# Gate and up products of four feed-forwards as seven half-size block products in place of eight, with the activations kept in float32 until the down product

## The chip, the cores and the metric

The kernel runs on one NeuronCore of one Trainium2 chip. A core has TensorE (PE, with its weight loads as PEld), VectorE (DVE), ScalarE (ACT), GpSimd (POOL), SyncE (SP, which here only issues DMAs) and 16 DMA engines. The engines run their own instruction queues in order and wait for each other by semaphores. The metric is the time of one execution on the device, in microseconds (us).

## What is computed

A gMLP layer and a dilated-attention layer are followed by a two-layer block whose four feed-forwards are called (layer, i): (0, 0), (0, 1), (1, 0), (1, 1). With T = 512 tokens, D = 1024 features and a hidden width of 2816 each feed-forward is

```python
def swiglu(x, w_gu, w_down):
    g, u = jnp.split(x @ w_gu, 2, axis=-1)      # w_gu: 1024 x 5632
    return (jax.nn.silu(g) * u) @ w_down        # w_down: 2816 x 1024

x = layer_norm_2(DN_ALPHA * x + 0.5 * swiglu(x, ffn_w_gu[layer, 0], ffn_w_down[layer, 0]), ...)
```

Attention mixers (mla after (0, 0), nsa after (1, 0)) stand between them, and a small stage of compressed keys and values stands between (0, 1) and (1, 0). All is float32.

## The kernel before, in words

**Products.** Every large product is made of matmuls on pairs "high" and "low": the high part is the value rounded to TensorE's fp32r form (written by ScalarE with `ACT.Copy`), the low part is value minus high (written by VectorE with a subtract). `mm3` issues three matmuls for one 128 x 128 weight tile: high x high, low x high, high x low. The stationary operand of a matmul is loaded anew each time.

**Weights.** `weight_panels` lists all weights as panels of up to 128 x 2048 in the order in which they are used. SP loads panel g into `RAW[g % 2]` once panel g - 2 has been split (L585). `prepare(g)` on ScalarE (L1330) and VectorE (L1710) splits panels in order into a ring of two homes (`w_high`, `w_low`), or, for the panels next to a row stage, into `edge_high`, `edge_low`.

**A feed-forward.** `xt_high` and `xt_low` hold the tokens' features turned, 8 tiles of 128 features x 512 tokens. The gate columns come in five chunks of 512 (two panels each: 4 output tiles x 8 feature tiles x 3 = 96 matmuls of 512 tokens), each followed by the up chunk of the same size; a last pair of panels ("last") holds 256 gate and 256 up columns. ScalarE takes silu of a gate bank into `gate_rows` (L1582), VectorE multiplies it with the up bank (L2070), ScalarE writes `hidden_high` (L1588) and VectorE `hidden_low` (L2073) at once. `down` multiplies them with 11 panels of the down weights.

**Starts.** Before a feed-forward stands a row stage: 4 tiles of 128 tokens are normalised, turned by TensorE and split. In three of the four feed-forwards `edge_product` begins the first product on the first 256 tokens with matmuls of 256 columns (L607 to L610), while the later tiles are still in work; 96 such matmuls come after the last tile is split (`xt_ready` of tile 3). Feed-forward (1, 0) follows the compressed stage instead: its first product runs whole, then `compress_out` issues a few small matmuls, and TensorE waits for ScalarE's copy of their result (`cmp_kept`, L1658).

**Order.** No scheduler: the program text of each engine's block is its order. GpSimd before only issues DMAs, takes roots of single columns (L2265) and scales a bias (L2383).

## Time and profile before

| What | Value |
|---|---|
| Time, median of 3 runs | 2964.39 us (2963.52 to 2964.39) |
| Span of the profiled execution | 2961.8 us |
| TensorE busy | 2919.8 us, 99% |
| Weight loads busy | 2421.4 us, 82% |
| VectorE busy | 1227.6 us, 41% |
| ScalarE busy | 1047.1 us, 35% |
| GpSimd busy | 101.4 us, 3% |
| Chain that ended last | 92% on TensorE |

The span of the profiled execution is 2.6 us under the median of the runs; no other time is given for it. Busy time is the time in which at least one instruction of the engine is in flight; matmuls overlap, so the cost of one in a stream is the distance between starts, not its own duration.

### The profile page before, as it was taken

To read this page: it belongs to the slowest core of one execution; us is meant where nothing else is said; L and a number is where in the kernel's file an instruction comes from. 1 tells how busy PE (TensorE), PEld (TensorE's weight loads), DVE (VectorE), ACT (ScalarE), POOL (GpSimd) and SP (SyncE) were. 2 spreads that over 40 slices of the span, in tenths; PEclk is the share of its full clock that TensorE was granted. 3 is DMA by queue.
4 is the path that set the end of the run, shared out by engine and by line. 5 is a ranking of instruction groups with operands and counts; after the bars stand their busy time and mean duration, and the time that the engine had idled before them with its cause. 6 is when DMAs were issued, how large, how long until landed. Compare 5 with 4: busy or idle time off the path is not lost.

```text
span 2961.8 us, 35864 instructions
## 1 busy us (share of the span) xinstructions
PE 2919.8 (99%) x15356; PEld 2421.4 (82%) x15356; DVE 1227.6 (41%) x1703; ACT 1047.1 (35%) x1749; POOL 101.4 (3%) x153
## 2 busy tenths in 40 slices
PE   7999999999999999999999999999999999999998
PEld 6888888788888788888868888888888886788887
DVE  4364342343333743333664333162332458633223
ACT  3323333444444332222473222133222248532221
POOL 1000000020000000000100000010000011000000
PEclk9999999999999999999999999999999999999999
DMA  5432322222222233323303323253332330123321
GB/s 195 140 102 95 102 89 99 84 67 79 79 80 75 93 99 100 99 93 101 95 23 107 100 86 99 100 145 114 100 100 100 80 106 1 58 100 100 100 100 71
DMA packets 145261, 278.18 MB, mean 94 GB/s; under 512 B 29578, under 2 KB 45114, under 8 KB 144976
## 3 DMA queue, kind: packets, MB, share of 16 engines
q1 hardware_dynamic: 136064, 247.17, 26.0%
q0 software_dynamic: 9040, 28.73, 3.0%
q8 instruction: 121, 1.98, 0.3%
q14 instruction: 36, 0.29, 0.0%
HBM read 271.56 MB, written 4.25 MB: 93 GB/s over the span
## 4 chain that ended last, share of the span: by engine, by line
PE 92%; DVE 4%; ACT 1%; issue 1%; DMA 1%; POOL 0%; SPq 0%; POOLq 0%; DVEq 0%; ACTq 0%
PE bank L596 26%; PE bank L598 26%; PE bank L597 26%; PE bank L734 2%; PE bank L607 1%; PE bank L610 1%; PE bank L609 1%; PE bank L822 1%; PE bank L790 1%; PE bank L754 1%; PE bank L806 1%; PE bank L743 1%; PE bank L715 1%; PE bank L968 0%; DMA cmp_pos_t<-in_cmp_pos 0%
## 5 line engine op out<-in xcount | busy, mean ns | idle before, releaser
L1710 DVE TENSOR_TENSOR w_low<-raw,w_high 128x2048 fp32r<-128x2048 f32 (+2 forms) x213 | 481.5, 2260 | 1190.4 <-ACT w_high L1330 1184.2
L596 PE MATMUL bank<-xt_high,w_high 128*128 128x512 f32 x2040 | 803.0, 394 | 1.6 <-DVE w_low L1710 1.2
L598 PE MATMUL bank<-xt_high,w_low 128*128 128x512 f32 x2040 | 794.7, 390 | 0.0
L597 PE MATMUL bank<-xt_low,w_high 128*128 128x512 f32 x2040 | 794.1, 389 | 0.0
L1330 ACT ACTIVATE w_high<-raw 128x2048 fp32r<-128x2048 f32 (+2 forms) x213 | 402.1, 1888 | 896.6 <-PE bank L598 892.3
L596 PEld LDWEIGHTS bank<-xt_high,w_high 128*128 128x128 f32 x2040 | 382.4, 187 | 89.5 <-issue 10.0
L598 PEld LDWEIGHTS bank<-xt_high,w_low 128*128 128x128 f32 x2040 | 382.3, 187 | 81.4
L597 PEld LDWEIGHTS bank<-xt_low,w_high 128*128 128x128 f32 x2040 | 382.7, 188 | 77.5
L596 PE MATMUL bank<-w_high,hidden_high 128*128 128x512 f32 x640 | 249.3, 390 | 0.0
L598 PE MATMUL bank<-w_high,hidden_low 128*128 128x512 f32 x640 | 249.0, 389 | 0.0
L597 PE MATMUL bank<-w_low,hidden_high 128*128 128x512 f32 x640 | 249.0, 389 | 0.0
L598 PEld LDWEIGHTS bank<-w_high,hidden_low 128*128 128x128 f32 x640 | 120.2, 188 | 25.1
L596 PEld LDWEIGHTS bank<-w_high,hidden_high 128*128 128x128 f32 x640 | 120.1, 188 | 24.9
L597 PEld LDWEIGHTS bank<-w_low,hidden_high 128*128 128x128 f32 x640 | 120.2, 188 | 24.7
L596 PE MATMUL bank<-w_high,xt_high 128*128 128x512 f32 (+1 forms) x336 | 131.0, 390 | 0.3 <-DVE w_low L1710 0.3
L597 PE MATMUL bank<-w_low,xt_high 128*128 128x512 f32 (+1 forms) x336 | 129.2, 384 | 0.0
L598 PE MATMUL bank<-w_high,xt_low 128*128 128x512 f32 (+1 forms) x336 | 129.2, 384 | 0.0
L1588 ACT ACTIVATE hidden_high<-gate_rows 128x512 fp32r<-128x512 f32 x88 | 55.1, 630 | 154.7 <-DVE gate_rows L2070 154.7
L2070 DVE TENSOR_TENSOR gate_rows<-bank,gate_rows 128x512 f32<-128x512 f32 x88 | 60.7, 689 | 115.5 <-PE bank L598 115.5
L1582 ACT ACTIVATE gate_rows<-bank 128x512 f32<-128x512 f32 x88 | 52.3, 598 | 151.7 <-PE bank L598 125.2
L2265 POOL TENSOR_TENSOR small<-small 128x1 f32<-128x1 f32 (+1 forms) x43 | 25.2, 585 | 2109.1 <-DVE small L1736 2070.8
L596 PEld LDWEIGHTS bank<-w_high,xt_high 128*128 128x128 f32 x336 | 79.4, 236 | 8.7 <-issue 1.1
(367 smaller groups left out, 3766.4 us busy)
## 6 DMA issues: line engine op xcount, KB each, us to landing
raw<-in_ffn_w_gu SPq DMA_DIRECT2D x80, 1024.0 KB, 5.1
raw<-in_ffn_w_down SPq DMA_DIRECT2D x44, 1024.0 KB, 5.0
raw<-in_b_w_in SPq DMA_DIRECT2D x40, 1024.0 KB, 5.1
raw<-in_a_w_in SPq DMA_DIRECT2D x24, 1024.0 KB, 5.2
raw<-in_a_w_out SPq DMA_DIRECT2D x8, 1024.0 KB, 5.0
raw<-in_ffn_w_gu SPq DMA_DIRECT2D x16, 512.0 KB, 4.8
raw<-in_w_out SPq DMA_DIRECT2D x5, 1024.0 KB, 4.9
raw<-in_w_mem_kv SPq DMA_DIRECT2D x4, 1024.0 KB, 5.2
```

The source lines that it names most:

```text
L596: pe.matmul(o, lh, rh, start=start, stop=False, skip_group_check=True)
L597: pe.matmul(o, lh, rl, start=False, stop=False, skip_group_check=True)
L598: return pe.matmul(o, ll, rh, start=False, stop=stop, skip_group_check=True)
L607: pe.matmul(o[:, cols], lh, rh[:, cols], start=a == 0 and i == 0 and kk == 0, stop=False, skip_group_check=True)
L609: pe.matmul(o[:, cols], lh, rl[:, cols], start=False, stop=False, skip_group_check=True)
L610: ins = pe.matmul(o[:, cols], ll, rh[:, cols], start=False, stop=a == 1 and i == 1 and kk == 3, skip_group_check=True)
L734: ins = pe.matmul(ps[4 + m % 2][:, a:b], q, k, start=True, stop=True)
L1330: act.activation(homes[n][0][:, 0:w], RAW[n % 2][:, 0:w], ACT.Copy).then_inc(sem["w_high_ready"], step("w_high_ready", n))
L1582: act.activation(G[:, j, :], ps[j][:], ACT.Silu).then_inc(sem["gate_read"], step("gate_read", (f, c, j)))
L1588: ins = act.activation(HTH[:, 4 * c + j, :], G[:, j, :], ACT.Copy)
L1710: dve.tensor_tensor(homes[n][1][:, 0:w], RAW[n % 2][:, 0:w], homes[n][0][:, 0:w].bitcast(F32), ALU.subtract).then_inc(sem["w_low_ready"], ...
L2070: dve.tensor_tensor(G[:, j, :], ps[bank + j][:], G[:, j, :], ALU.mult).then_inc(sem["up_read"], step("up_read", (f, c, j)))
```

## The change

The first 256 hidden columns of each feed-forward are computed as before (panels "first", moved from the end to the front). Each further unit of 256 hidden columns (10 units, `UNITS` = 11) takes the product of the unit's gate and up weights with the tokens as a 2 x 2 block product: the tokens cut in features 0 to 511 and 512 to 1023 and in tokens 0 to 255 and 256 to 511; the weights cut in the same feature halves and in gate and up. Seven block products of half size (`FACTORS`) in place of eight give the four result blocks. For that:

- four sums and differences of token blocks are made once per feed-forward (three on VectorE, sum 3 on GpSimd in `differences`), and split into high and low;
- four differences of weight blocks are made in every unit on GpSimd (`put`), two of them in place in `RAW`, so a panel stays there until they are made and split;
- each of the seven weight factors (128 x 1024) is split by `high(q)` on ScalarE and `low(q)` on VectorE into one of five slots, used again once the product five earlier is done;
- products add to each other in three PSUM banks per unit; ScalarE copies a bank between two products (snapshot), VectorE adds snapshots and banks, silu and the multiplication follow in halves of 256 tokens;
- the hidden activations stay in float32 and are split after the units, from the last unit on (`hidden_high(u)`, `hidden_low(u)`).

The core of the diff:

```diff
-        for c in range(5):
-            deep(("gate", l, i, c), w, 512 * c, 512)
-            deep(("up", l, i, c), w, D_FF + 512 * c, 512)
         for k0 in (0, 4):
-            add(("last", l, i), [(0, 4, 512, 256, rows(w, k0, 4, 2560, 256)),
-                                 (256, 4, 512, 256, rows(w, k0, 4, D_FF + 2560, 256))])
+            add(("first", l, i), [(0, 4, 512, 256, rows(w, k0, 4, 0, 256)),
+                                  (256, 4, 512, 256, rows(w, k0, 4, D_FF, 256))])
+        for u in range(1, UNITS):
+            for c0 in (256 * u, D_FF + 256 * u):
+                add(("unit", l, i, u), [(0, 8, 256, 256, rows(w, 0, 8, c0, 256))])
...
+        g, up = ids["unit", *f, u]
+        gate_raw, up_raw = RAW[g % 2], RAW[up % 2]
+        slot = FFN[f]["slots"][q % 5]
+        src = (gate_raw[:, 0:1024], gate_raw[:, 1024:2048], DIFF2, gate_raw[:, 0:1024], up_raw[:, 0:1024],
+               up_raw[:, 1024:2048], DIFF4)[n]
...
+    DIFF2, DIFF4 = (SPARE[i][:, 0:4, 256:512] for i in range(2))
...
+            if g - 2 in unit_of:
+                l, i, u, half = unit_of[g - 2]
+                sp.wait_ge(sem["factor_ready"], at("factor_ready", ((l, i), u, 5 if half else 3)))
+                if half == 0:
+                    sp.wait_ge(sem["differences"], at("differences", ((l, i), u, 6)))
...
+            moving = (tokens(0, 0), tokens(4, 0), sums(2), sums(1), sums(3), sums(4), tokens(4, 256))
+            for q in range(FACTORS * (UNITS - 1)):
+                u, n = 1 + q // FACTORS, q % FACTORS
+                A, B, C = unit_banks(u)
+                bank = (A, B, A, C, A, C, A)[n]
+                pe.wait_ge(sem["factor_ready"], at("factor_ready", (f, u, n)))
+                if n == 0 and u >= 3:
+                    pe.wait_ge(sem["unit_gated"], at("unit_gated", (f, u - 2, 1)))
...
+                    pe.wait_ge(sem["snapped"], at("snapped", (f, u, n - 2)))
+                if u == 1 and 2 <= n < 6:
+                    pe.wait_ge(sem["sum_split"], at("sum_split", (f, SUM_ORDER[n - 2])))
+                slot = tiles["slots"][q % 5]
+                for j in range(2):
+                    o = bank[:, 256 * j:256 * j + 256]
+                    for kk in range(4):
+                        a = 256 * kk + P * j
+                        opens = n in (0, 1, 3) and j == 0 and kk == 0
+                        ins = mm3(o, slot[:, a:a + P], slot[:, 1024 + a:1024 + a + P], *moving[n](kk), opens,
+                                  n in (1, 5, 6) and j == 1 and kk == 3)
+                ins.then_inc(sem["unit_done"], step("unit_done", (f, u, n)))
...
+            def high(q):
...
+                g, up = ids["unit", l, i, u]
+                if n in (0, 1):
+                    act.wait_ge(sem[f"panel_loaded{g % 2}"], at(f"panel_loaded{g % 2}", g))
+                elif n == 5:
+                    act.wait_ge(sem[f"panel_loaded{up % 2}"], at(f"panel_loaded{up % 2}", up))
+                else:
+                    act.wait_ge(sem["differences"], at("differences", (f, u, n)))
+                if q < 5:
+                    act.wait_ge(sem["product_done"], at("product_done", ("panel", tiles["before"][q])))
+                else:
+                    act.wait_ge(sem["unit_done"], at("unit_done", (f, 1 + (q - 5) // FACTORS, (q - 5) % FACTORS)))
+                act.activation(dst, src, ACT.Copy).then_inc(sem["factor_high"], step("factor_high", (f, u, n)))
...
+            prepare(ids["first", l, i][-1])
+            high(0)
+            high(1)
+            for n in SUM_ORDER:
+                if n == 3:
+                    act.wait_ge(sem["sum3_ready"], at("sum3_ready", f))
+                else:
+                    act.wait_ge(sem["sum_ready"], at("sum_ready", (f, n)))
+                act.activation(tiles["sum_high"][n][:], tiles["sum"][n][:],
+                               ACT.Copy).then_inc(sem["sum_high"], step("sum_high", (f, n)))
+            for j in range(2):
+                act.wait_ge(sem["product_done"], at("product_done", ("acc", ("first", l, i), j)))
+                act.activation(SNAP[j][:].rearrange("p a n -> p (a n)"), ps[j][:], ACT.Silu).then_inc(sem["gate_read"], step("gate_read", (f, j)))
+            high(3)
...
+                    to, bank = {0: (0, A), 2: (1, A), 3: (3, C), 4: (2, A)}[n]
+                    act.activation(SNAP[to][:].rearrange("p a n -> p (a n)"), bank[:],
+                                   ACT.Copy).then_inc(sem["snapped"], step("snapped", (f, u, n)))
+                if n == 2:
+                    act.wait_ge(sem["gate_summed"], at("gate_summed", (f, u)))
+                    act.activation(SNAP[0][:], SNAP[0][:], ACT.Silu).then_inc(sem["unit_gated"], step("unit_gated", (f, u, 0)))
+                if n == 6:
...
+                def x(high, k0, t0):
...
+                dve.wait_ge(sem["xt_ready"], at("xt_ready", (s, TT - 1)))
+                s1, s2, s4 = (tiles["sum"][n][:] for n in (1, 2, 4))
+                link(dve.tensor_tensor(s1, x(True, 0, 256), x(True, 4, 256), ALU.add))
+                link(dve.tensor_tensor(s1, s1, x(False, 0, 256), ALU.add))
+                end(1, s1, x(False, 4, 256), ALU.add)
+                link(dve.tensor_tensor(s2, s1, x(True, 0, 0), ALU.subtract))
+                end(2, s2, x(False, 0, 0), ALU.subtract)
+                link(dve.tensor_tensor(s4, x(True, 4, 0), s2, ALU.subtract))
+                end(4, s4, x(False, 4, 0), ALU.add)
...
+            token_sums()
+            for n in SUM_ORDER:
+                dve.wait_ge(sem["sum_high"], at("sum_high", (f, n)))
+                dve.tensor_tensor(tiles["sum_low"][n][:], tiles["sum"][n][:], tiles["sum_high"][n][:].bitcast(F32),
+                                  ALU.subtract).then_inc(sem["sum_split"], step("sum_split", (f, n)))
...
+                    dve.wait_ge(sem["unit_done"], at("unit_done", (f, u, n)))
+                if n == 1:
+                    dve.wait_ge(sem["snapped"], at("snapped", (f, u, 0)))
+                    dve.tensor_tensor(SNAP[0][:], bank(B), SNAP[0][:], ALU.add).then_inc(sem["gate_summed"], step("gate_summed", (f, u)))
+                if n == 5:
+                    dve.wait_ge(sem["snapped"], at("snapped", (f, u, 2)))
+                    link(dve.tensor_tensor(SNAP[1][:], bank(C), SNAP[1][:], ALU.add))
+                    dve.wait_ge(sem["unit_gated"], at("unit_gated", (f, u, 0)))
+                    dve.tensor_tensor(tiles["hidden"][u][:, :, 0:256], SNAP[1][:], SNAP[0][:],
+                                      ALU.mult).then_inc(sem["unit_hidden"], step("unit_hidden", (f, u, 0)))
+                    dve.wait_ge(sem["snapped"], at("snapped", (f, u, 4)))
+                    link(dve.tensor_tensor(SNAP[2][:], SNAP[2][:], SNAP[3][:], ALU.add))
+                if n == 6:
...
-        prepare(ids["gate", 1, 0, 0][-1] + 1)
+        prepare(ids["first", 1, 0][-1])
         dve.wait_ge(sem["kv_kept"], at("kv_kept"))
-        ffn(1, 0)
+        dve.wait_ge(sem["cmp_halves_done"], at("cmp_halves_done"))
+        ffn(1, 0, "l02")
...
+            high, low, out = XTH, XTL, FFN[f]["sum"][3][:]
+            pool.wait_ge(sem["xt_ready"], at("xt_ready", (s, TT - 1)))
+            link(pool.tensor_tensor(out, high[:, 0:4, 0:256].bitcast(F32), high[:, 0:4, 256:512].bitcast(F32), ALU.subtract))
+            link(pool.tensor_tensor(out, out, low[:, 0:4, 0:256].bitcast(F32), ALU.add))
+            pool.tensor_tensor(out, out, low[:, 0:4, 256:512].bitcast(F32),
+                               ALU.subtract).then_inc(sem["sum3_ready"], step("sum3_ready", f))
...
+            for u in range(1, UNITS):
+                g, up = ids["unit", l, i, u]
+                b11, b21 = deep(RAW[g % 2][:, 0:1024]), deep(RAW[g % 2][:, 1024:2048])
+                b12, b22 = deep(RAW[up % 2][:, 0:1024]), deep(RAW[up % 2][:, 1024:2048])
+                def put(n, dst, a, b):
+                    pool.tensor_tensor(dst, a, b, ALU.subtract).then_inc(sem["differences"], step("differences", (f, u, n)))
+                    pool.wait_ge(sem["differences"], at("differences", (f, u, n)))
...
+                pool.wait_ge(sem["factor_ready"], at("factor_ready", (f, u, 0)))
+                put(3, b11, b12, b11)
+                if u == 1:
+                    pool.wait_ge(sem["product_done"], at("product_done", ("panel", ids["first", l, i][1])))
+                    pool.wait_ge(sem["sum_ready"], at("sum_ready", (f, 1)))
+                else:
+                    pool.wait_ge(sem["factor_ready"], at("factor_ready", (f, u - 1, 2)))
+                put(2, DIFF2, b22, b11)
+                put(4, b12, b22, b12)
+                if u > 1:
+                    pool.wait_ge(sem["factor_ready"], at("factor_ready", (f, u - 1, 6)))
+                put(6, DIFF4, b21, DIFF2)
```

**Start of (1, 0), ScalarE.** In the program before, the rows from the copy of the compressed keys (`cmp_keys`) on are:

```order
L1657 ACTIVATE cmp_keys<-bank 128x32 [waits cmp_done]
L1658 ACTIVATE cmp_values<-bank 128x128
L1582 ACT_TABLE_LOAD [waits product_done]
L1582 ACTIVATE gate_rows<-bank 128x512 [waits kv_kept]
L1582 ACTIVATE gate_rows<-bank 128x512 [waits product_done] x3
L1330 ACTIVATE w_high_63<-raw_62 128x2048 [waits product_done,panel_loaded1]
```

In the changed program they are:

```order
L1838 ACTIVATE cmp_keys<-bank 128x32 [waits cmp_done]
L1839 ACTIVATE cmp_values<-bank 128x128
L1712 ACTIVATE w_high_63<-raw_61 128x1024 [waits product_done,panel_loaded0,kv_kept]
L1712 ACTIVATE w_low_65<-raw_61 128x1024 [waits product_done,panel_loaded0]
L1730 ACTIVATE sum_high_161<-sum_10_163 128x1024 [waits sum_ready]
L1730 ACTIVATE sum_high_164<-sum_10_166 128x1024 [waits sum_ready]
L1730 ACTIVATE sum_high_167<-sum_10_169 128x1024 [waits sum3_ready]
L1730 ACTIVATE sum_high_170<-sum_10_172 128x1024 [waits sum_ready]
L1734 ACT_TABLE_LOAD
L1734 ACTIVATE snapshot_253<-bank 128x512 [waits product_done]
L1734 ACTIVATE snapshot_254<-bank 128x512 [waits product_done]
```

`raw_61` here is the gate panel of unit 1 (factors 0 and 1), `sum_...` are the token sums in the order 2, 1, 3, 4, and L1734 is the silu of the gate banks of the first product. The split of factor 0 stands right behind the compressed stage's copies, and the sums' splits stand between it and the first silu.

**The same place, VectorE.** Before, behind the compressed stage:

```order
L1710 TENSOR_TENSOR w_low_66<-raw_61,w_high_64 128x2048 [waits w_high_ready]
L1710 TENSOR_TENSOR w_low_65<-raw_62,w_high_63 128x2048 [waits w_high_ready,kv_kept]
L1710 TENSOR_TENSOR w_low_66<-raw_61,w_high_64 128x2048 [waits w_high_ready]
L2070 TENSOR_TENSOR gate_rows<-bank,gate_rows 128x512 [waits gate_read,product_done] x4
L2073 TENSOR_TENSOR hidden_low<-gate_rows,hidden_high 128x2048 [waits hidden_high]
```

In the changed program:

```order
L1894 TENSOR_TENSOR edge_low_kv<-raw_61,edge_high_kv 128x2048 [waits w_high_ready]
L1894 TENSOR_TENSOR w_low_66<-raw_62,w_high_64 128x2048 [waits w_high_ready]
L2249 TENSOR_TENSOR w_high_63<-raw_61,w_high_63 128x1024 [waits factor_high,cmp_halves_done,kv_kept]
L2249 TENSOR_TENSOR w_low_65<-raw_61,w_low_65 128x1024 [waits factor_high]
L2265 TENSOR_TENSOR sum_10_166<-xt_high 128x1024 [waits xt_ready]
L2266 TENSOR_TENSOR sum_10_166<-sum_10_166,xt_low 128x1024 [waits dve_step]
L2260 TENSOR_TENSOR sum_10_166<-sum_10_166,xt_low 128x1024 [waits dve_step]
L2268 TENSOR_TENSOR sum_10_163<-sum_10_166,xt_high 128x1024 [waits sum_ready]
L2260 TENSOR_TENSOR sum_10_163<-sum_10_163,xt_low 128x1024 [waits dve_step]
L2270 TENSOR_TENSOR sum_10_172<-xt_high,sum_10_163 128x1024 [waits sum_ready]
L2260 TENSOR_TENSOR sum_10_172<-sum_10_172,xt_low 128x1024 [waits dve_step]
L2284 TENSOR_TENSOR sum_low_162<-sum_10_163,sum_high_161 128x1024 [waits sum_high,sum_ready]
```

The seven sums (L2260 to L2270) stand behind the low parts of factors 0 and 1, each of which waits for its high part (`factor_high`), which ScalarE writes in the rows above.

**Within a unit, GpSimd.** Before, nothing stands here. In the changed program each unit has four rows, and the fifth is the next unit's first:

```order
L2555 TENSOR_TENSOR raw_62<-raw_61,raw_62 128x1024 [waits factor_ready,panel_loaded0,differences]
L2555 TENSOR_TENSOR xt_spare_54<-raw_61,raw_62 128x4x256 [waits factor_ready,differences]
L2555 TENSOR_TENSOR raw_61<-raw_61 128x1024 [waits differences]
L2555 TENSOR_TENSOR xt_spare_55<-raw_62,xt_spare_54 128x4x256 [waits factor_ready,differences]
L2555 TENSOR_TENSOR raw_62<-raw_61,raw_62 128x1024 [waits factor_ready,panel_loaded0,differences]
```

These are `put(3)`, `put(2)`, `put(4)`, `put(6)`: `raw` are the unit's gate and up panels, `xt_spare` the spare places DIFF2 and DIFF4. The first waits for the up panel and for factor 0's low part.

## Rows read from the trace of the kernel before

**Rows 1.** The page: busy us, share of the span, instructions.
```profile
span 2961.8 us, 35864 instructions
...
PE 2919.8 (99%) x15356; PEld 2421.4 (82%) x15356; DVE 1227.6 (41%) x1703; ACT 1047.1 (35%) x1749; POOL 101.4 (3%) x153
```

**Rows 2.** Windows, gate and up of (0, 0): us, PE, PEld, DVE, ACT, POOL, clock, DMA.
```profile
1085.00:1262.00 177.00, 177.00 (x783) 146.61 (x782) 56.17 (x36) 51.36 (x49) 0.00 (x0) 1.00 0.30 95
```

**Rows 3.** Timeline, TensorE, 512 columns: start us, us, what; 24 starts apart.
```profile
1100.06 0.39 PE L596 MATMUL bank<-xt_high,w_high 128*128 128x512 f32 x1
...
1105.50 0.39 PE L596 MATMUL bank<-xt_high,w_high 128*128 128x512 f32 x1
```

**Rows 4.** Timeline, TensorE, 256 columns, 83 starts apart, and one weight load.
```profile
1060.84 0.28 PE L607 MATMUL bank<-xt_high,edge_high_s 128*128 128x256 f32 x1
...
1070.79 0.28 PE L610 MATMUL bank<-xt_high,edge_low_s 128*128 128x256 f32 x1
...
1070.67 0.19 PEld L610 LDWEIGHTS bank<-xt_high,edge_low_s 128*128 128x128 f32 x1
```

**Rows 5.** Groups by form, ScalarE and VectorE: busy us, mean ns, idle before.
```profile
L1330 ACT ACTIVATE w_high<-raw 128x1024 fp32r<-128x1024 f32 x2 | 2.1, 1057 | 0.0
...
L1582 ACT ACTIVATE gate_rows<-bank 128x512 f32<-128x512 f32 x88 | 52.3, 598 | 151.7 <-PE bank L598 125.2 <-PE bank L610 26.5
...
L1710 DVE TENSOR_TENSOR w_low<-raw,w_high 128x1024 fp32r<-128x1024 f32 x2 | 2.4, 1220 | 0.0
...
L2070 DVE TENSOR_TENSOR gate_rows<-bank,gate_rows 128x512 f32<-128x512 f32 x88 | 60.7, 689 | 115.5 <-PE bank L598 115.5
...
L2031 DVE TENSOR_TENSOR b_o<-b_o,b_o 128x512 f32<-128x512 f32 x8 | 5.5, 692 | 0.3
```

**Rows 6.** The page, DMA issues: KB each, median us to landing.
```profile
raw<-in_ffn_w_gu SPq DMA_DIRECT2D x80, 1024.0 KB, 5.1
...
raw<-in_ffn_w_gu SPq DMA_DIRECT2D x16, 512.0 KB, 4.8
```

**Rows 7.** Groups by form, GpSimd, whole span.
```profile
L2265 POOL TENSOR_TENSOR small<-small 128x1 f32<-128x1 f32 x40 | 22.1, 552 | 2023.4 <-DVE small L1736 1985.0 <-DVE small L1743 38.3
...
L2383 POOL TENSOR_SCALAR n_bias<-nsa_dist 128x512 f32<-128x512 f32 x12 | 18.4, 1539 | 113.9 <-DVE small L1889 100.2 <-PE bank L610 13.4
```

**Rows 8.** The same in 2440 to 2520; VectorE in 2450.7 to 2452.6, in 2519 to 2525.
```profile
L2383 POOL TENSOR_SCALAR n_bias<-nsa_dist 128x512 f32<-128x512 f32 x8 | 12.5, 1562 | 100.3 <-DVE small L1889 100.2
...
L1903 DVE TENSOR_SCALAR n_p<-n_p,small,nsa_gates 128x128 f32<-128x128 f32 x2 | 1.3, 633 | 0.0
...
L1903 DVE TENSOR_SCALAR n_p<-n_p,small,nsa_gates 128x128 f32<-128x128 f32 x2 | 0.7, 344 | 0.0
```

**Rows 9.** Timeline, start of feed-forward (0, 0): VectorE, TensorE.
```profile
1061.80 1.29 DVE L1729 TENSOR_TENSOR xt_low<-bank,xt_high 128x512 fp32r<-128x512 f32 x2 [2.45 <-ACT xt_high L1343]
...
1074.75 0.28 PE L610 MATMUL bank<-xt_high,edge_low_s 128*128 128x256 f32 x1
...
1074.87 0.40 PE L596 MATMUL bank<-xt_high,w_high 128*128 128x512 f32 x1
```

**Rows 10.** Timeline, start of feed-forward (1, 0): TensorE, ScalarE.
```profile
2023.66 1.10 PE L1242 MATMUL bank<-cmp_w_t,cmp_hidden 128*128 128x64 f32 x8
...
2025.22 0.50 PE L596 MATMUL bank<-xt_high,w_high 128*128 128x512 f32 x1 [0.46 <-ACT cmp_values L1658]
...
2024.90 0.27 ACT L1658 ACTIVATE cmp_values<-bank 128x128 f32<-128x128 f32 x1
...
2025.19 1.28 ACT L1582 ACT_TABLE_LOAD   x1
```

**Rows 11.** Windows around an idle TensorE, columns as in rows 2.
```profile
410.00:415.00 5.00, 2.35 (x11) 1.59 (x9) 3.09 (x4) 3.06 (x5) 0.55 (x1) 1.00 0.00 0
...
415.00:420.00 5.00, 4.73 (x18) 3.96 (x19) 3.68 (x7) 2.98 (x7) 0.55 (x1) 0.66 0.00 0
```

More of the change, by code:

```diff
@@ L371, in build @@
             freed_by[g] = ids[y][-5 if len(ids[y]) > 4 else -4]
-    ring = [g for g in range(len(panels)) if g not in homes]
+    home("kv", ids["first", 1, 0][0], 28, 36)
+    freed_by[ids["first", 1, 0][0]] = ids["kv_a"][1]
+    unit_of = {g: (l, i, u, half) for (l, i) in FFN for u in range(1, UNITS)
+               for half, g in enumerate(ids["unit", l, i, u])}
+    ring = [g for g in range(len(panels)) if g not in homes and g not in unit_of]
     for n, g in enumerate(ring):
@@ L1040, in ffn @@
-            product(("last", l, i), 4, [(ps[setA[j]][:], feature(512, j * P, XTH, XTL)) for j in range(4)],
-                    lambda j: pe.wait_ge(sem["gate_read"], at("gate_read", (f, 4, j))))
+            tiles = FFN[f]
+            jobs = [(ps[setA[j]][:], feature(512, j * P, XTH, XTL)) for j in range(4)]
+            if s:
+                edge_product(("first", l, i), jobs, s)
+            else:
+                product(("first", l, i), 4, jobs, lambda j: None, ahead=ahead)
+            if between:
+                between()
@@ L1593, in _ @@
+            for u in range(3, UNITS):
+                hidden_high(u)
         ffn(0, 0)
```

271 lines of the change are left out of this document (201 added, 70 removed).

## The prediction

> **What bounds the kernel now.** I read the page first: TensorE is busy for 2919.8 of 2961.8 us, VectorE for 41% of the span, GpSimd for 3% [rows 1]. Then a window inside the gate and up products of (0, 0): 177 us, TensorE busy for all of it, clock 1.00, VectorE and ScalarE each busy for under a third [rows 2]. So in these stages matmuls alone set the time, and what a matmul costs is the distance from one start to the next. The timeline gives it: with 512 columns 24 starts take 5.44 us, 226.7 ns each [rows 3]; with 256 columns, in the edge products, 83 starts take 9.95 us, 119.9 ns each, every matmul with a fresh weight load of 0.19 us that overlaps its neighbours [rows 4]. The reader should see that two halves cost 239.8 ns where one whole costs 226.7: halving a matmul is not free, and the gain of seven products for eight is first cut by that.
>
> **TensorE in the units.** A unit of 256 hidden columns now takes 4 output tiles x 8 feature tiles x 3 = 96 matmuls of 512 columns, 96 x 226.7 ns = 21.76 us. In the changed kernel it takes 7 products x 2 x 4 x 3 = 168 of 256 columns, 168 x 119.9 ns = 20.14 us. That is 1.62 us less, not the eighth of 2.7 us. There are 10 units in each of 4 feed-forwards: -64.8 us. The first 256 columns and the down product keep their matmuls. One block product lasts 24 x 119.9 ns = 2.88 us.
>
> **Splits and sums within a unit, costed at nothing.** ScalarE: seven high parts of 1024 at 1.06 us and six PSUM reads or silus at 0.60 us, 11.0 us of 20.14. VectorE: seven low parts at 1.22 us and five adds or multiplications of 512 at 0.69 us, 12.0 us [rows 5]. Both fit beside TensorE. The tight place is the snapshot: the bank of product n goes on being added to in product n + 2, so ScalarE has one product, 2.88 us, to wake and copy it in 0.60 us; its longest other task in that time is a silu and a high part, 1.66 us. It holds. A factor's slot comes free four products ahead of its use, 11.5 us for 0.60 + 1.06 + 1.22 us of work. The hidden splits left for the end (eight low parts, 9.8 us of VectorE) lie beside the first two down panels, 48 matmuls x 226.7 ns = 10.9 us each. The panels land in 5.1 us; pieces whose rows are 256 columns long already exist and land in 4.8 us for half the size, two to a panel [rows 6], so I keep 5.1.
>
> **GpSimd, the new cover that can fail.** Each unit has four `put`, and they close a loop: four puts, then SP may load the next gate panel (5.1 us), then high and low of factor 0 (1.06 + 1.22 us), and only then the next unit's first put. With 0.8 us that I allow for six semaphores between, the loop is 4p + 8.2 us. It is hidden while it is under 20.14 us, so p may be up to 3.0 us. No row shows a GpSimd tensor_tensor of 1024 elements. The nearest rows are 0.55 us for one element and 1.54 us for 512 with one input [rows 7]: 1.94 ns for an element, 2.54 us for 1024. Below, p can't be under the 1.54 us of half the size; above, if two inputs cost twice the slope, 4.5 us. I take 2.54, the same line continued, 2.6 with its own semaphore: the loop is 18.6 us and hidden. At 4.5 us it would be 26.2 us, and the kernel some 210 us slower than now. The Trainium skill (GPSIMD Engine Reference, Elementwise — side-by-side cycle accounting) gives 4497 ns for 2048 float32 elements with two inputs; halving what is over the one-element 0.55 us is an estimate of 2.5 us, and the sum by it is the same.
>
> What VectorE and GpSimd do to each other is to be seen in the nsa stage. Four short VectorE operations on 128 elements last 633 ns beside a GpSimd bias scaling and 344 ns without one; GpSimd's own mean is 1562 ns there against 1539 ns over all [rows 7, 8]. So VectorE gives way by 0.29 us an operation and GpSimd hardly. Within a unit VectorE has 8 us to spare, and nothing more is charged.
>
> **The three starts behind a row stage.** At the start of (0, 0) VectorE ends the last split of tokens at 1063.1 and TensorE's 96 matmuls of 256 columns run to 1074.8, 11.7 us later [rows 9]. In the changed kernel two block products follow (5.8 us), and the third needs, from VectorE and in this order: two low parts, seven sums of 1024 each waiting for the one before (1.22 us and 0.07 that I allow for each semaphore, 9.0), four low parts of sums, two multiplications, two low parts. That is 8 x 1.22 + 9.0 + 1.4 = 20.2 us against 17.5 of TensorE's: 2.7 us of stall. GpSimd makes sum 3 and its first put in these 10 us; at 0.29 us for each of eight VectorE operations that is 2.3 us more. I take 5.0 us for each, 15 us.
>
> **The start of (1, 0).** Here ScalarE's program has the split of factor 0 behind the compressed stage's copies, which end at 2025.2, the moment at which TensorE now goes on with the up product [rows 10]. The tokens have been ready long before, but VectorE's sums are queued behind the low part of factor 0, and ScalarE's first silu behind all sum splits. From 2025.2 on: high 1.06, the same 20.2 us on VectorE, 21.3 us, against 5.8 us of TensorE's work: 15.5 us of stall. In it TensorE idles from about 5.2 to 15.5 us for the silu (sums to 12.5, high part 1.1, a table load of 1.28, silu 0.6) and product 1 follows. After a stretch of 5 us with TensorE at 2.35 us of work the granted clock is 0.66 in the next 5 us [rows 11], between its two levels of 1.2 and 2.4 GHz; most of that falls inside the wait. With 1 us for it and 1 us for GpSimd's company: 17.5 us.
>
> **Sum.** -64.8 + 15 + 17.5 = -32.3 us. Profiled span and median differ by 2.6 us [rows 1], which doesn't change: 2964.4 - 32.3 = 2932 us.
>
> **The rivals.**
> - GpSimd's loop decides (3 in 10). For it: the whole loop has 1.5 us of slack, p is read off a one-input operation, and while puts run VectorE has low parts with two inputs in SBUF, which rows 8 don't show. If each put has to let half or all of a 1.22 us operation pass, p is 3.2 to 3.8 us and the unit 21.0 to 23.4 us. From p = 3.2 on the gain is gone (40 x (21.0 - 21.76) + 32.5 = about 0); at 3.5 us the unit is 22.2 us and the kernel 40 x 0.44 + 32.5 = 50 us slower, 3014 us. Against it: GpSimd's mean in rows 8. The Trainium skill (SBUF — State Buffer, Who interferes with whom) says that a VectorE instruction with two SBUF inputs contends with a GpSimd instruction that reads SBUF; no row here shows that pair.
> - The starts are covered (1 in 10): if the chained sums follow closer and sum splits overlap, the three starts cost about 1 us each and only (1, 0) stays, at some 10 us: 2964.4 - 64.8 + 13 = 2913 us, 2900 at the least. Against it: the order on VectorE is fixed, and 20.2 us is pure work.
> - The starts cost more (1 in 10): if VectorE's sums are slowed by half beside GpSimd, 5 us more each, 20 us in all: 2952 us.
> - That matmuls of 256 columns from `unit_slot` cost other than those of the edges: each ns is 168 x 40 = 6.7 us. Rows 4 show the same shapes and forms; it is inside the range.
>
> **How the numbers follow.** The forecast has 5 in 10 and its own range is 2918 to 2945 us. What a measurement of this kernel tells from no change is about 0.2%, 6 us. Of GpSimd's 3 in 10 a tenth of a chance (0.03) ends faster, 0.03 the same, 0.24 slower; of the dear starts 0.02 the same. Faster 0.71, same 0.05, slower 0.24. The range reaches down into the covered starts and up to p = 3.5: 2903 to 3012 us; outside are 0.12 of GpSimd's case and some 0.05 below and between.
>
> **What the profile after would show.** Starts of L664 to L666 119.9 ns apart; a unit every 20.1 us with TensorE busy throughout (if it is 21 us or more, the chain of waits should name GpSimd's L2555 or the gate panel's load in front of ScalarE's high part of factor 0); GpSimd's puts at 2.5 to 2.7 us; three gaps of 3 to 5 us before the third block product, and one of 15 to 18 us in two pieces after the compressed stage. The prediction is wrong if puts are over 3.0 us, if snapshots come later than the product after next, or if the sums take other than 9 us.

## The result, and the profile after

The changed kernel takes 3048.89 us (median of 4 runs, 3047.79 to 3049.26) against 2964.39 us before: a ratio of 1.0286, 95% interval 1.0272 to 1.0301. It is 84.5 us slower, where 32 us less were forecast. The page of after, in the form of [rows 1]:

```profile
span 3047.5 us, 43223 instructions
...
PE 2891.3 (95%) x18236; PEld 2534.4 (83%) x18236; DVE 1655.5 (54%) x2087; ACT 1265.2 (42%) x2081; POOL 585.4 (19%) x325
...
PE 64%; DVE 13%; DMA 7%; issue 6%; POOL 6%; ACT 3%; POOLq 0%; SPq 0%; DVEq 0%; ACTq 0%
```

TensorE has less work, as forecast, but is no longer the whole chain that ended last (last row): a third of that is VectorE, GpSimd, transfers and hand-overs. Windows inside the units of (0, 1) and of (1, 0), columns as in [rows 2]:

```profile
1660.00:1840.00 180.00, 168.97 (x1356) 167.41 (x1355) 112.32 (x97) 82.51 (x105) 88.23 (x32) 0.97 0.28 92
2094.00:2274.00 180.00, 167.61 (x1351) 166.22 (x1351) 114.83 (x97) 82.57 (x104) 87.30 (x32) 0.97 0.28 93
```

TensorE idles for 11 to 12 of 180 us, at a granted clock of 0.97. No engine but TensorE is busy for two thirds of it, so what sets the time is a loop of dependences. The waits name its members (the third row is the four starts, not the loop; columns: who waited for whom, us in all, times, longest):

```profile
POOL raw L2555 <- DMA raw<-in_ffn_w_gu: 430.0, 36, 17.5
ACT snapshot L1752 <- DVE hidden L2312: 103.8, 36, 2.9
PE bank L664 <- ACT snapshot L1734: 57.0, 4, 16.6
PE bank L664 <- ACT snapshot L1752: 53.3, 36, 2.7
```

The chain through one unit gives its order (start, us, what):

```profile
1705.68 5.37 DMA raw<-in_ffn_w_gu
...
1711.17 3.19 POOL raw L2555
...
1714.43 2.42 POOL xt_spare L2555
...
1716.87 1.07 ACT w_low L1712
...
1718.10 2.24 issue
1720.34 0.69 DVE snapshot L2310
...
1721.09 2.06 issue
1723.15 0.69 DVE snapshot L2315
...
1725.01 0.68 DVE hidden L2318
1725.69 1.14 DVE w_high L2249
1726.83 1.15 DVE w_low L2249
...
1727.99 6.36 DMA raw<-in_ffn_w_gu
```

The **up** panel is loaded, GpSimd makes differences 3 and 2, ScalarE and VectorE split factor 2, VectorE adds snapshots and splits factors up to 5, and only then may SP load the next up panel: 1727.99 - 1705.68 = 22.3 us. From the load at 1660.25 to the one at 1840.74 there are eight units, 22.56 us each, and the chain holds no TensorE work between them. The loop through the gate panel is hardly shorter: in this unit the low part of factor 0 ends at 1710.50, 0.55 us before the up panel lands. The two stretches of "issue" over 2 us are VectorE operations that had started and lasted: the low part of factor 2 and L2312, both with two SBUF inputs, while GpSimd was at a difference. By form (mean ns):

```profile
L2555 POOL TENSOR_TENSOR xt_spare<-raw,xt_spare 128x1024 f32<-128x1024 f32 x40 | 130.1, 3253 | 3.1
L2555 POOL TENSOR_TENSOR raw<-raw,raw 128x1024 f32<-128x1024 f32 x40 | 114.9, 2872 | 441.5 <-DMA raw<-in_ffn_w_gu 430.0 <-DVE w_high L2249 11.3
L2312 DVE TENSOR_TENSOR hidden<-snapshot,snapshot 128x512 f32<-128x512 f32 x40 | 80.8, 2020 | 1.4
L2249 DVE TENSOR_TENSOR w_low<-xt_spare,w_low 128x1024 fp32r<-128x1024 f32 x32 | 58.6, 1833 | 97.2 <-ACT w_low L1712 97.2
L2307 DVE TENSOR_TENSOR snapshot<-bank,snapshot 128x512 f32<-128x512 f32 x40 | 27.3, 684 | 0.0
```

L2312 takes 2.02 us for 512 elements; L2307, with one input in PSUM, 0.68. The start of (0, 0) on the timeline, where [rows 9] show before:

```profile
1061.17 1.29 DVE L1912 TENSOR_TENSOR xt_low<-bank,xt_high 128x512 fp32r<-128x512 f32 x2 [2.45 <-ACT xt_high L1462]
...
1066.85 3.42 DVE L2265 TENSOR_TENSOR sum<-xt_high 128x1024 f32<-128x1024 f32 x1
...
1076.99 1.23 DVE L2268 TENSOR_TENSOR sum<-sum,xt_high 128x1024 f32<-128x1024 f32 x1
...
1062.60 3.24 POOL L2540 TENSOR_TENSOR sum<-xt_high 128x1024 f32<-128x1024 f32 x1 [6.28 <-DVE xt_low L1912]
...
1089.78 0.55 PE L664 MATMUL bank<-xt_high,w_low 128*128 128x256 f32 x1 [12.51 <-ACT snapshot L1734]
...
1096.37 0.39 PE L664 MATMUL bank<-sum_high,w_high 128*128 128x256 f32 x1 [1.53 <-DVE w_high L2249]
...
1311.07 0.40 PE L664 MATMUL bank<-w_high,hidden_high 128*128 128x512 f32 x1
```

Six of VectorE's seven sums last 3.2 to 3.4 us, and so does the low part of factor 1 ahead of them (3.42 us at 1063.50); only the sum at 1076.99, which begins in a pause of GpSimd, lasts 1.23. Product 2 starts at 1096.37 where unhindered TensorE would be there 17.5 us after 1062.5, so 16.4 us late. At (1, 0) it starts at 2092.05, ScalarE having ended the compressed stage's copies at 2063.3: 28.7 - 5.8 = 22.9 us late.

**Where the 84.5 us are.** I measure each stage from the row of the last low parts of tokens (1061.17 above) to the first down matmul (1311.07; before, from 1061.80 to 1292.50, 230.7). Unhindered, product 2 to the down product takes 5 x 2.88 + 9 x 20.14 = 195.7 us; here 1311.07 - 1096.37 = 214.7. The stage of (1, 0) holds the compressed stage too. In us, from the timelines of all kernels:

| kernel | (0, 0) to product 2 | product 2 to down | stage (1, 0) |
|---|---|---|---|
| before | | (whole: 230.7) | 274.9 |
| after | 35.2 | 214.7 | 301.5 |
| e1_tiny_puts | 27.1 | 195.9 | 273.5 |
| e3_one_input | 30.0 | 199.8 | 283.1 |
| e4_short_up | 35.2 | 207.4 | 295.3 |
| e5_short_gate | 35.2 | 204.7 | 295.2 |
| e11_short_both | 35.2 | 199.7 | 283.4 |
| e13_vector_sum3 | 33.1 | 213.9 | 307.5 |
| e9_ahead_only | 35.2 | 214.1 | 288.5 |
| e6_vector_puts | 32.1 | 197.7 | 280.1 |
| e7_all_vector | 29.4 | 197.7 | 283.5 |
| e8_ahead | 29.4 | 197.4 | 265.5 |
| e10_starts | 20.7 | 204.0 | 266.0 |

From product 2 to the down product the other feed-forwards stay within 3 us of (0, 0), but for e3_one_input (202.6 to 203.5), e5_short_gate at (1, 0) (210.0) and e13_vector_sum3 in layer 1 (217.7, 218.0). In the changed kernel the units lose 19.0 to 20.2 us in each feed-forward, 78 in all; three starts 16.4 each, 49; (1, 0) 22.9. -64.8 + 78 + 49 + 23 = +85.

### The profile page after: what moved, and what is told of

It reads as the page before. It is cut to its first block, busy times and chain, and to the rows that moved or that the text cites. A ratio compares the mean times of both kernels' runs of the same rounds, so it can differ in the third digit from the quotient of the medians.

```text
span 3047.5 us, 43223 instructions
## 1 busy us (share of the span) xinstructions
PE 2891.3 (95%) x18236; PEld 2534.4 (83%) x18236; DVE 1655.5 (54%) x2087; ACT 1265.2 (42%) x2081; POOL 585.4 (19%) x325
## 4 chain that ended last, share of the span: by engine, by line
PE 64%; DVE 13%; DMA 7%; issue 6%; POOL 6%; ACT 3%; POOLq 0%; SPq 0%; DVEq 0%; ACTq 0%
PE bank L664 17%; PE bank L666 17%; PE bank L665 17%; DMA raw<-in_ffn_w_gu 6%; POOL raw L2555 3%; POOL xt_spare L2555 3%; DVE w_low L2249 2%; DVE w_high L2249 2%; PE bank L802 2%; PE bank L890 1%; PE bank L858 1%; DVE sum L2260 1%; PE bank L874 1%; PE bank L822 1%; PE bank L811 1%
## 5 line engine op out<-in xcount | busy, mean ns | idle before, releaser
L1894 DVE TENSOR_TENSOR w_low<-raw,w_high 128x2048 fp32r<-128x2048 f32 (+1 forms) x132 | 296.1, 2243 | 663.5 <-ACT w_high L1450 657.1
L1450 ACT ACTIVATE w_high<-raw 128x2048 fp32r<-128x2048 f32 (+1 forms) x132 | 247.2, 1874 | 529.4 <-PE bank L666 522.9
L664 PE MATMUL bank<-xt_high,w_high 128*128 128x512 f32 (+1 forms) x1128 | 407.8, 361 | 3.7 <-DVE w_high L2249 2.8
L666 PE MATMUL bank<-xt_high,w_low 128*128 128x512 f32 (+1 forms) x1128 | 402.6, 357 | 0.0
L665 PE MATMUL bank<-xt_low,w_high 128*128 128x512 f32 (+1 forms) x1128 | 399.2, 354 | 0.0
L664 PEld LDWEIGHTS bank<-xt_high,w_high 128*128 128x128 f32 x1128 | 213.3, 189 | 40.7 <-issue 12.5
L666 PEld LDWEIGHTS bank<-xt_high,w_low 128*128 128x128 f32 x1128 | 216.6, 192 | 31.2
L665 PEld LDWEIGHTS bank<-xt_low,w_high 128*128 128x128 f32 x1128 | 213.7, 189 | 27.1
L664 PE MATMUL bank<-sum_high,w_low 128*128 128x256 f32 x512 | 150.2, 293 | 26.5 <-ACT snapshot L1752 26.5
L664 PE MATMUL bank<-sum_high,w_high 128*128 128x256 f32 x512 | 148.6, 290 | 22.0 <-ACT snapshot L1752 20.0
L666 PE MATMUL bank<-sum_high,w_low 128*128 128x256 f32 x512 | 148.9, 291 | 0.0
L666 PE MATMUL bank<-sum_high,w_high 128*128 128x256 f32 x512 | 147.0, 287 | 0.0
```

What stands on the lines that cost most here:

```text
L664: pe.matmul(o, lh, rh, start=start, stop=False, skip_group_check=True)
L665: pe.matmul(o, lh, rl, start=False, stop=False, skip_group_check=True)
L666: return pe.matmul(o, ll, rh, start=False, stop=stop, skip_group_check=True)
L1450: act.activation(homes[n][0][:, 0:w], RAW[n % 2][:, 0:w], ACT.Copy).then_inc(sem["w_high_ready"], step("w_high_ready", n))
L1894: dve.tensor_tensor(homes[n][1][:, 0:w], RAW[n % 2][:, 0:w], homes[n][0][:, 0:w].bitcast(F32), ALU.subtract).then_inc(sem["w_low_ready"], ...
```

## The experiments

**The cause named: GpSimd's differences.** e1_tiny_puts cuts them to one column (factors 2 and 6 are then split from a block of tokens, so the values are others), e3_one_input makes them copies with one SBUF input (differences left out):

```diff
-pool.tensor_tensor(dst, a, b, ALU.subtract)
+pool.tensor_tensor(dst[:, :, 0:1], a[:, :, 0:1], b[:, :, 0:1], ALU.subtract)   # e1
+pool.tensor_scalar(dst, a, 1.0, None, ALU.mult)                                # e3
```

> The changed kernel, with GpSimd's four weight differences of each unit cut to one column, and factors 2 and 6 split from a fixed block of tokens: the arithmetic of the differences is left out, every wait and every other instruction stays. Theory (GpSimd's puts, by their own length and by what VectorE loses beside them, set the unit): in the changed kernel a unit takes 22.56 us (eight of them from 1660.25 to 1840.74); here it takes TensorE's 20.14, and factor 2's low part 1.22 us in place of 1.8 to 2.5: 40 x 2.4 = 97 us less, and some 20 us less at the starts, 2925 to 2950 us. Rival (the order of the program and the loads set the unit): over 21.5 us a unit, over 3005 us.

> The changed kernel, with each put a copy of its first operand by tensor_scalar (one SBUF input) in place of a subtraction of two: the differences are wrong, nothing else changes. Theory A (any GpSimd instruction that reads SBUF holds off a VectorE tensor_tensor with two SBUF inputs until it ends): VectorE's operations beside a put still last 2 us and more, and the unit stays at 22 us or more, total within 30 us of 3049. Theory B (only two-input operations of both engines collide): they last 1.22 us, the unit 20.1 to 20.6 us, total 2950 to 2975 us.

e1: 2939.11 us, ratio 0.9917 (0.9889 to 0.9946). As its theory said, the units run at TensorE's pace (195.9 us): 110 us come back through GpSimd's differences alone. e3: 2977.38, ratio 1.0046 (1.0030 to 1.0062). It falls between its two theories, 2 us over the range of B. GpSimd's operation is no shorter (2.98 and 2.82 us), but VectorE's low parts of factors 2 and 6 last 1.22 us again (1.83 and 1.68 in after); L2312 still takes 1.45 us where it takes 2.02 in after and the like operation L2318, free of GpSimd, 0.68. A unit takes 21.2 us, not 20.1. So how long GpSimd takes counts, and so does what it does to VectorE.

**The loads.** Only 1 of 8 pieces of the up panel, the gate panel or both is loaded; the rest of the factors is what stood in the buffer.

```diff
-for c0 in (256 * u, D_FF + 256 * u):
-    add(("unit", l, i, u), [(0, 8, 256, 256, rows(w, 0, 8, c0, 256))])
+for c0, nk in ((256 * u, 8), (D_FF + 256 * u, 1)):      # e4; 1, 8 in e5; 1, 1 in e11
+    add(("unit", l, i, u), [(0, nk, 256, 256, rows(w, 0, nk, c0, 256))])
```

> The changed kernel, with only the first 128 of 1024 rows of each unit's up panel loaded (the rest of the buffer is stale). Theory (the loop runs through the up panel: its load, put 3, put 2, factors 2 to 5 in order on VectorE, release of its buffer): the load of 5.3 to 6.4 us falls by 3 us or more and the unit with it, to between 20.1 and 20.6 us, total 2950 to 2975 us. Rival (the loop of the prediction, through the gate panel): no change within 10 us of 3049.

> The changed kernel, with only the first 128 of 1024 rows of each unit's gate panel loaded. Theory (loop through the up panel): within 10 us of 3049, apart from a little for less traffic beside the up panel's load. Rival (the loop of the prediction, through the gate panel): the unit falls to about 20.2 us, 2950 to 2975 us.

> The changed kernel (differences on GpSimd) with only an eighth of both panels of a unit loaded, so that both land in some 2.6 us; the rest of the arithmetic is the same, on what stands in the buffers. Short up alone gave units of 21.7 us, short gate alone 21.1. Theory A (two loops of nearly equal length, through the up panel and through the gate panel, each with a load, GpSimd's stretched differences and hand-overs; cutting one leaves the other): with both cut the unit falls to TensorE's 20.1 to 20.4 us and the kernel to 2975 to 2995 us. Theory B (GpSimd and VectorE hold each other up by themselves, loads or not): the unit stays at 21 us or more, 3005 us or more.

e4: 3025.24, ratio 1.0208 (1.0178 to 1.0238), units of 21.7 us, 50 us over the theory's range: with the up panel early the loop through the gate panel decides. The chain of e4 shows it:

```profile
1714.84 5.01 DMA raw<-in_ffn_w_gu
...
1720.96 1.24 DVE w_low L2249
...
1722.36 2.41 POOL raw L2555
...
1724.85 3.28 POOL xt_spare L2555
...
1736.38 5.44 DMA raw<-in_ffn_w_gu
```

The gate panel lands, factor 0's low part is made, then differences 3 and 2, and VectorE's queue up to the low part of factor 3, which frees the panel at 1714.83, 2.4 us after the fourth difference has ended at 1712.40; 21.5 us in all. e5: 3011.89, ratio 1.0163 (1.0134 to 1.0193), units of 21.1 to 21.2 us; I had expected next to nothing, since the chain of after runs through the up panel. That was wrong, though the chain of e5 runs through the up panel as well: its load takes 5.0 us where the eight of after took 5.9 on average, and difference 3, with factor 1's low part no longer beside it, 2.40 where it took 2.96. That is 1.4 us, the whole gain of a unit. e11: 2980.22, ratio 1.0057 (1.0037 to 1.0077), units at 20.2 us, although the stretched operations are all still there:

```profile
1660.00:1840.00 180.00, 179.26 (x1483) 178.09 (x1483) 144.18 (x110) 93.58 (x116) 91.75 (x33) 1.00 0.08 25
...
L2555 POOL TENSOR_TENSOR xt_spare<-raw,raw 128x1024 f32<-128x1024 f32 x40 | 130.6, 3264 | 10.3 <-DVE sum L2260 7.5
```

This is theory A. So there are two loops of nearly equal length, each a sum of three kinds of terms: a load, GpSimd's and VectorE's stretched operations, and VectorE's queue. Taking GpSimd's operations out (e1) or both loads down (e11) gets them to TensorE's 20.14 us or next to it; one load (e4, e5) or most of VectorE's stretch (e3) does not.

**The pair by itself.** e12_pairs leaves the whole computation out: six operations of each engine in each stretch, on tiles of their own.

> No feed-forward at all: only VectorE and GpSimd operations of 1024 float32 elements side by side, six of each in a stretch, on tiles that nothing else touches. My theory (two engines that read two SBUF inputs each share what feeds them): VectorE's tensor_tensor alone 1.2 us, GpSimd's alone 2.4 us; side by side both about 3.2 us; VectorE with one PSUM input 0.7 us for 512 columns beside it, unslowed; VectorE tensor_tensor beside GpSimd's one-input tensor_scalar (2.8 us) under 1.6 us. Rival (the slowing comes from the loads, ScalarE or the chains of this kernel): side by side as alone.

By form; L52 and L93 are alone, then the pairs L58 with L97, L63 with L101, L67 with L105, L73 with L113, L77 with L117; L109 is alone:

```profile
L52 DVE TENSOR_TENSOR vec_out<-vec_a,vec_b 128x1024 f32<-128x1024 f32 x6 | 6.9, 1219 | 9.6 <-ACT bank L42 9.6
L93 POOL TENSOR_TENSOR gp_out<-gp_a,gp_b 128x1024 f32<-128x1024 f32 x6 | 13.8, 2342 | 8.0 <-DVE vec_out L52 8.0
L58 DVE TENSOR_TENSOR vec_out<-vec_a,vec_b 128x1024 f32<-128x1024 f32 x6 | 17.6, 3001 | 13.8 <-POOL gp_out L93 13.8
L97 POOL TENSOR_TENSOR gp_out<-gp_a,gp_b 128x1024 f32<-128x1024 f32 x6 | 19.8, 3329 | 0.1
L63 DVE TENSOR_TENSOR vec_out<-bank,vec_b 128x512 f32<-128x512 f32 x12 | 7.3, 679 | 2.3 <-POOL gp_out L97 2.3
L101 POOL TENSOR_TENSOR gp_out<-gp_a,gp_b 128x1024 f32<-128x1024 f32 x6 | 13.9, 2355 | 0.1
L67 DVE TENSOR_SCALAR vec_out<-vec_a 128x1024 f32<-128x1024 f32 x6 | 14.4, 2470 | 6.7 <-POOL gp_out L101 6.7
L73 DVE TENSOR_TENSOR vec_out<-vec_a,vec_b 128x1024 f32<-128x1024 f32 x6 | 9.4, 1635 | 16.5 <-POOL gp_out L109 16.5
L113 POOL TENSOR_SCALAR gp_out<-gp_a 128x1024 f32<-128x1024 f32 x6 | 18.2, 3064 | 0.2 <-POOL gp_out L109 0.2
L109 POOL TENSOR_SCALAR gp_out<-gp_a 128x1024 f32<-128x1024 f32 x6 | 16.4, 2770 | 0.2 <-POOL gp_out L105 0.2
L77 DVE TENSOR_TENSOR vec_out<-vec_a,vec_b 128x512 f32<-128x512 f32 x6 | 14.4, 2468 | 9.0 <-POOL gp_out L113 9.0
L117 POOL TENSOR_TENSOR gp_out<-gp_a,gp_b 128x1024 f32<-128x1024 f32 x6 | 16.6, 2793 | 0.1
```

Without loads, chains or other engines, VectorE goes from 1.22 to 3.00 us and GpSimd from 2.34 to 3.33. They take turns: 1.15 + 2.31 us, the distances from start to start alone, are 3.46, and a pair took 19.8 / 6 = 3.3. Half the elements on VectorE hardly help (2.47 us, L77), while a GpSimd operation of 256 elements beside a VectorE one of 1024 holds it up for less (L81, 1.65 us): an operation waits for the other engine's operation, not for a share of it. With one PSUM input nothing happens to either. The rival is out; of my theory's figures only the last is missed, by little (L73, 1.64 us for under 1.6). This kernel ran once.

**The differences and sums on VectorE.** e6_vector_puts has VectorE make the four differences of a unit, e7_all_vector also sum 3, e13_vector_sum3 sum 3 only (the differences of unit 1, not in this cut, stand in the start: 3 ahead of the sums' low parts, 2 behind them, 4 and 6 ahead of factor 4's):

```diff
 for q in range(count):
     ...
         low(q + 5)
+    if u < UNITS - 1:
+        for m in {3: (3, 2), 4: (4,), 5: (6,)}.get(n, ()):
+            put(u + 1, m)          # dve.tensor_tensor(dst, a, b, ALU.subtract)
```

> The changed kernel with the four differences of each unit made by VectorE (4 x some 1.22 us) in place of GpSimd; sum 3 of each feed-forward stays on GpSimd. My theory (a GpSimd difference of 2.4 us, stretched to 3.2 us by VectorE's two-SBUF-input operations and stretching them in turn, makes the loop over the two panels longer than TensorE's 20.14 us): VectorE then has 12.0 + 4.9 = 16.9 us of 20.14, the loop shrinks by some 7 us, a unit takes 20.1 to 20.3 us, VectorE's factor lows last 1.22 us, and the kernel is 100 to 115 us faster than the changed one, 2930 to 2950 us. Rival (the loop is too long because of the two panel loads and the hand-overs between engines, whoever makes the differences): the unit stays above 21.3 us and the kernel above 2990 us. Rival (VectorE becomes the bound): idle TensorE waits for VectorE's lows, unit over 20.6 us, 2965 us or more.

> As the kernel with VectorE's differences, and sum 3 of the tokens is made by VectorE too: nothing of the feed-forwards is left on GpSimd. My theory of the starts (VectorE's sums of 1.22 us last 3.3 us because they run beside GpSimd's sum 3 and first difference): all sums last 1.22 us; VectorE gets three operations more (3.9 us) and loses three stretches of 2.1 us (6.3 us), so each start is some 2.4 us shorter than in the kernel before in this series, 8 to 12 us in all over four. Rival (the sums are slow for another reason, such as the chained read of what was just written): they stay at over 2 us, and the kernel is 12 us or more slower than the one with sum 3 on GpSimd.

> The changed kernel with sum 3 of the tokens on VectorE and the four differences of each unit left on GpSimd. My theory of the starts (each has four to seven VectorE operations stretched from 1.2 to 3.3 us by GpSimd's sum 3): the sums last 1.23 us, each of the four starts is 4 to 8 us shorter, the units stay at 22.5 us: 3015 to 3032 us. Rival (the starts are long because of GpSimd's first differences, which come after the sums in either kernel): within 10 us of 3048.9.

e6: 2966.92, ratio 1.0014 (1.0005 to 1.0023). TensorE is busy for all of the window, and the units are back at its pace:

```profile
1660.00:1840.00 180.00, 180.00 (x1474) 178.77 (x1473) 144.38 (x143) 98.89 (x121) 0.00 (x0) 1.00 0.34 113
```

Its theory of the units holds, but it misses its range by 17 us in the starts: two of the first unit's differences are now ahead of the low parts that product 2 waits for (32.1 us, e1 has 27.1). e7: 2961.35, ratio 0.9993 (0.9984 to 1.0003), 5.6 us faster than e6 with three operations more on VectorE, where 8 to 12 were expected. The three starts gain 2.7 us each, as in the theory; at (1, 0), where GpSimd made sum 3 of e6 long before it was wanted, the three operations only lengthen the stage, by 3.4 us. e13: 3047.13, ratio 1.0283 (1.0262 to 1.0303); I had expected 17 to 34 us less than the changed kernel and got 2, as the rival had it. Its start shows why:

```profile
1068.00 1.23 DVE L2266 TENSOR_TENSOR sum<-sum,xt_low 128x1024 f32<-128x1024 f32 x1
...
1079.34 11.12 DVE L2289 TENSOR_TENSOR sum_low<-sum,sum_high 128x1024 fp32r<-128x1024 f32 x4
...
1079.48 3.31 POOL L2552 TENSOR_TENSOR xt_spare<-raw,raw 128x1024 f32<-128x1024 f32 x1 [12.60 <-DVE sum L2275]
```

All sums but the first (3.43 us, beside difference 3) last 1.23 us, but GpSimd's differences 2, 4 and 6 now come beside the four low parts of sums: 11.1 us for four where e7 takes 4.6. The contention had only moved.

**The order at the starts.** In e9_ahead_only (on the changed kernel) and e8_ahead (on e7) ScalarE does the first high parts of (1, 0) before it waits for the compressed stage; in e10_starts (on e8) VectorE and ScalarE make only what product 2 wants first.

```diff
+ffn(1, 0, "ahead")     # high(0), high(1), high parts of the sums
 act.wait_ge(sem["cmp_done"], at("cmp_done"))
 ...
-ffn(1, 0)
+ffn(1, 0, "behind")
```
```diff
 low(3)
 low(2)
-put(1, 4)
-put(1, 6)
-low(4)
+split(1); put(1, 4); sum3(); low(4); split(3); split(4); put(1, 6)    # e10, on one line here
```

> As the kernel with everything on VectorE, and in feed-forward (1, 0) ScalarE's high parts of factors 0 and 1 and of the four token sums stand ahead of its wait for the compressed stage rather than behind it, so that this work lies beside the compressed stage's matmuls. My theory of that start (some 23 us of stall because the factor's split waits for the copies of the compressed stage): 14 to 20 us faster than the kernel without this edit, in all 2900 to 2925 us, below both kernels. Rival (the stall there comes from the clock and from matmuls that are slow behind a row stage, not from the order on ScalarE): less than 5 us.

> The changed kernel with GpSimd's differences as they are, and only the order of ScalarE at the start of (1, 0) changed (high parts of factors 0 and 1 and of the sums ahead of the wait for the compressed stage). My theory: the stall of some 23 us at that start goes for the most part, the units stay at 22.5 us: 3024 to 3034 us. Rival (the units of (1, 0) start earlier but the loop over the panels is then just as late, since the first units wait for GpSimd and the loads): under 8 us, 3041 us or more.

> The last kernel of the series before (all differences and sums on VectorE, ScalarE's work of (1, 0) ahead) waits 4.4 to 6.1 us before product 2 of each of the four feed-forwards, since VectorE makes all sums, all four low parts of sums and two differences before the low part of factor 2. Here VectorE makes only what product 2 wants first (sums 1, 2, 4, one operation of sum 3, difference 3, low part of sum 2, difference 2, low parts of factors 3 and 2), the rest of sum 3 and the other low parts behind it; ScalarE's silus and snapshots stand accordingly. My theory (the starts are bound by VectorE's order up to product 2): the wait before product 2 falls from 4.4 to 6.1 us to under 2 us, some of it comes back before products 4 or 5; 10 to 25 us faster than 2943, 2918 to 2933 us, 1.0 to 1.5% below the kernel before the change. Rival (what bounds the start is VectorE's whole work up to product 5, 30 us in any order): within 5 us of 2943.

e9: 3033.40, ratio 1.0237 (1.0222 to 1.0252), stage (1, 0) 13.0 us shorter, just in its range. e8: 2943.42, ratio 0.9934 (0.9918 to 0.9951), that stage 18.1 us shorter than in e7; the gain is the one expected (14 to 20 us), but the total misses its range by 18 us, since e7, from which it starts, was itself slower than I had counted on. e10: 2934.88, ratio 0.9903 (0.9886 to 0.9919), the fastest of all and 28.6 us under the kernel before in the same comparison. It lies between theory and rival, 2 us over the theory's range: product 2 starts 8.7 us earlier, but 6.6 us come back, 4.9 of them before product 4:

```profile
1082.94 0.39 PE L664 MATMUL bank<-sum_high,w_high 128*128 128x256 f32 x1 [1.70 <-DVE w_high L2258]
...
1093.90 0.55 PE L664 MATMUL bank<-sum_high,unit_slot 128*128 128x256 f32 x1 [4.94 <-ACT snapshot L1757]
...
1092.26 1.06 ACT L1712 ACTIVATE w_low<-xt_spare 128x1024 fp32r<-128x1024 f32 x1 [2.66 <-DVE xt_spare L2306]
```

I put ScalarE's high part of factor 6 ahead of the snapshot that product 4 waits for, and difference 6 last on VectorE. By these rows a better order might be worth up to those 4.9 us in each start; it was not tried.

## Why the prediction was wrong

- **Right: TensorE's price.** With GpSimd out of the way a unit takes 20.1 us (e1, e6: 180.00 of 180 us busy), and the change in the units is the -64.8 us of the sum. In these two kernels splits and snapshots on ScalarE are hidden, too.
- **Wrong: "the loop is 4p + 8.2 us".** This is the step that failed: it let the four differences free the panel and found the loop hidden. The gate panel also waits for the low part of factor 3, which VectorE ends 2.4 us after the fourth difference (1702.77 against 1700.37 in after), and the up panel for that of factor 5. The loop that decides in after runs through the up panel: load 5.4, difference 3, difference 2, high part 1.1, then 10 us of VectorE's queue, 22.56 us a unit on average; the one through the gate panel follows at 21.5 (e4). My step charged VectorE's work by its busy time ("VectorE has 8 us to spare") and not as a stretch of the loop. p itself came out at 2.79 us over the four (3.25, 2.87, 2.56, 2.49), for which my formula gives 19.4 us and a hidden loop; so even with the right p it would have said faster. Alone such an operation takes 2.34 us (e12), near the 2.54 that I took.
- **Wrong: "VectorE gives way by 0.29 us an operation and GpSimd hardly".** [rows 8] are a one-input GpSimd operation beside short VectorE ones with one tensor input, two of them on either side and not four. The pair of two-input operations costs VectorE 1.8 to 2.2 us each (e12, and the sums of the start). In the loop of the chain above it is 0.8 us on difference 3 (3.19 against 2.40 in e5), 1.2 on the low part of factor 2 and 1.4 on L2312: 3.4 of 22.3 us. By this sum 18.9 us would be left, hidden under 20.14; that is an estimate, no run has GpSimd's differences at full speed with nothing stretched. Without 3.4 us of load (e11: 2.0 for 5.4) it is 18.9 as well, and there e11 shows the units at 20.2 us. This was the first rival's mechanism, given 3 in 10, and 3014 us by a p of 3.5 us. It was right in kind, with too short a loop behind it and too cheap starts beside it. The Trainium skill (SBUF — State Buffer, Who interferes with whom), cited there, says which pairs contend, and e12 agrees for L58 and L63.
- **Wrong in size: the three starts, 5.0 us each.** They are 16.4 us. GpSimd's company was charged at 2.3 us; six sums and one low part last 3.2 to 3.4 us in place of 1.22, which is 14.7 us. The other VectorE work took 1 us less than my 20.2. That is the 11.4 us of the miss. The seven sums take 21.2 us, not 9. The rival of dear starts, given 1 in 10, had the cause and less than half of the size (5 us more each, for 11.4); e7, where nothing of this is on GpSimd, has all sums at 1.23 us.
- **Size nearly right: (1, 0), 17.5 us.** It is 22.9; four of its sums last 3.25 to 3.40 us, 8.3 us more where I had allowed 1. That the miss is only 5.4 is partly luck: the rest of the order was shorter than my 21.3 us by 0.9, and the 1 us for the clock was not needed, since product 2 starts as soon as VectorE's low part is there. e8 shows that its cause, ScalarE's order, was right (18.1 us back).
- **Within the sum:** -64.8 + 15 + 17.5 had no term for the units; 78 us were missing there, 34 at the starts, 5 at (1, 0).

## What to carry to other kernels

Before work goes to an idle engine, ask what it shares with the engine that is to be relieved, and price the pair: here GpSimd's differences stretched VectorE's own work by 1.8 us a unit (112.3 us in 180 and 22.56 us a unit in after, 110.0 and 20.14 in e1) and were stretched themselves by up to 0.9 us each. Of that 3.4 us lay on the loop in the unit shown, where VectorE does all four in 3.9 us beside TensorE (e6). A loop of dependences is as long as everything on its way, the queue in front of each member too; walk every buffer's way from load to release and not only the first that looks tight, and expect a second loop right behind the one you cut (e4). And where a prologue is serial, order it by what the next product wants.
